# A token-major query statistic moved from ahead of the attention items into three of them

## The reference, cut to what matters

```python
q = (rms_norm(c_q, g_cq) @ w_uq).reshape(b, l, MLA_HEADS, MLA_QK)
q = rope_tail(rms_norm(q, g_q_mla), cos, sin)
...
s = jnp.einsum('bqhd,bkhd->bhqk', q_blk, k, preferred_element_type=jnp.float32) * scale
s = jnp.where(mask[None, None], s, NEG)
p = jax.nn.softmax(s, axis=-1)
return jnp.einsum('bhqk,bkhd->bqhd', p.astype(v.dtype), v)
```

## Time and profile before

| what | us |
| --- | --- |
| median of 3 runs (lowest to highest) | 1388.16 (1387.38 to 1391.67) |
| the profiled execution, device time | 1393.52 |
| its span in the profile | 1391.6 |
| PE busy | 1334.9 (96%) |
| DVE busy | 966.0 (69%) |
| ACT busy | 736.4 (53%) |
| POOL busy | 462.4 (33%) |

### The profile page before, as it was taken

How to read it: one execution, slowest core, us unless ns; L and a number is a source line. 1 busy time by engine, 2 the same in 40 slices (tenths; PEclk the granted TensorE clock), 3 DMA queues, 4 the chain that set the end, 5 groups by cost and what they waited for, 6 DMA issues and landing times.

```text
span 1391.6 us, 29208 instructions
## 1 busy us (share of the span) xinstructions
PE 1334.9 (96%) x10776; PEld 1298.5 (93%) x10776; DVE 966.0 (69%) x1446; ACT 736.4 (53%) x1224; POOL 462.4 (33%) x492
## 2 busy tenths in 40 slices
PE   5999999999999999999999999999999969999997
PEld 5787699999999999999989999999998859999996
DVE  6767567664477677555655679997578786999844
ACT  5454645444444454444545456665446844766642
POOL 3532044321111443211636324333126563333310
PEclk9998999999999999999999999999999969999998
DMA  7440045555555555555525545554554426455451
GB/s 268 150 149 32 1 152 174 186 185 184 180 181 183 180 180 183 190 187 186 195 92 183 187 175 185 183 182 169 189 202 162 137 94 223 159 191 189 143 203 53
DMA packets 34508, 230.53 MB, mean 166 GB/s; under 512 B 3838, under 2 KB 4990, under 8 KB 10662
## 3 DMA queue, kind: packets, MB, share of 16 engines
q1 hardware_dynamic: 33652, 226.47, 46.8%
q10 hardware_dynamic: 770, 2.90, 0.6%
HBM read 228.17 MB, written 1.05 MB: 165 GB/s over the span
## 4 chain that ended last, share of the span: by engine, by line
PE 77%; issue 8%; DVE 6%; ACT 4%; POOL 4%; DMA 1%; POOLq 0%; DVEq 0%; ACTq 0%; SPq 0%
PE ps L378 25%; PE ps L379 25%; PE ps L380 25%; DVE wlo L343 2%; POOL xlo L468 2%; ACT whi L338 2%; POOL ssum L474 1%; PE ps L1085 1%; DMA raw<-w 1%; DVE rstd L442 1%; DVE work L1470 1%; POOL q_mla L1857 1%; DVE work L1441 0%; PE ps L422 0%; ACT work L1752 0%
## 5 line engine op out<-in xcount | busy, mean ns | idle before, releaser
L343 DVE TENSOR_TENSOR wlo<-raw,whi 128x1024 fp32r<-128x1024 f32 (+1 forms) x448 | 546.5, 1225 | 106.2 <-ACT whi L338 105.2
L378 PE MATMUL ps<-xhi,whi 128*128 128x256 f32 (+2 forms) x2064 | 586.5, 284 | 18.5 <-DVE wlo L343 13.9
L379 PE MATMUL ps<-xlo,whi 128*128 128x256 f32 (+2 forms) x2064 | 584.6, 283 | 0.0
L380 PE MATMUL ps<-xhi,wlo 128*128 128x256 f32 (+2 forms) x2064 | 583.5, 283 | 0.0
L338 ACT ACTIVATE whi<-raw 128x1024 fp32r<-128x1024 f32 (+1 forms) x448 | 448.5, 1008 | 141.2 <-PE ps L380 136.9
L378 PEld LDWEIGHTS ps<-xhi,whi 128*128 128x128 f32 x2064 | 391.9, 190 | 23.2 <-issue 15.9
L380 PEld LDWEIGHTS ps<-xhi,wlo 128*128 128x128 f32 x2064 | 392.3, 190 | 0.0
L379 PEld LDWEIGHTS ps<-xlo,whi 128*128 128x128 f32 x2064 | 389.9, 189 | 0.3
L378 PE MATMUL ps<-hhi,whi 128*128 128x256 f32 (+1 forms) x1184 | 338.0, 285 | 7.7 <-POOL hlo L1947 7.4
L380 PE MATMUL ps<-hhi,wlo 128*128 128x256 f32 (+1 forms) x1184 | 335.7, 283 | 0.0
L379 PE MATMUL ps<-hlo,whi 128*128 128x256 f32 (+1 forms) x1184 | 335.5, 283 | 0.0
(11 more groups left out here) (262 smaller groups left out, 1314.3 us busy)
## 6 DMA issues: line engine op xcount, KB each, us to landing
raw<-w SPq DMA_DIRECT2D x184, 1024.0 KB, 4.9
raw<-w SPq DMA_DIRECT2D x40, 768.0 KB, 4.2
h<-x_fm ACTq DMA_DIRECT2D x1, 1088.0 KB, 6.4
out_fm<-h SPq DMA_DIRECT2D x8, 128.0 KB, 2.0
ws<-ws_src ACTq DMA_DIRECT2D x1, 512.0 KB, 5.0
bs<-bs_rows ACTq DMA_DIRECT2D x1, 512.0 KB, 5.8
consts<-constants ACTq DMA_DIRECT2D x1, 508.0 KB, 9.7
q_fox<-decay_rows SPq DMA_DIRECT2D x1, 340.0 KB
```

What stands on the lines that cost most here:

```text
L343: nc.vector.tensor_tensor(wlo[:, j % HLR, 0:n], raw[:, slot, col:col + n], whi[:, j % HLR, 0:n].bitcast(F32), ALU.subtract).then_inc(wlo_d ...
L378: nc.tensor.matmul(o, hi, xh, start=start, stop=False)
L379: nc.tensor.matmul(o, hi, xl, start=False, stop=False)
L380: mm = nc.tensor.matmul(o, lo, xh, start=False, stop=stop)
```

## The change

PE no longer makes the statistic ahead of the items. `q_stats(k)` makes one group, inside `turn(j)` of items 2, 3 and 4 (the third to fifth item, steps 4, 5 and 6), after the waits of `turn` and before its transposes, and writes bank 6 (columns 256 to 279) instead of bank 7. `turn(5)`, which writes bank 6 again in step 7, waits for the roots. The first `spread` waits only for the roots before (n_root 3). On ACT the two roots come in step 6, between `turned(4)` and `high`. On DVE the six scaling instructions come in step 7, behind `k_normed` and ahead of `low`. The number of products, roots and scaling instructions stays the same.

```diff
-            q_stats()
...
+                if j in (2, 3, 4):
+                    q_stats(j - 2)
+                if j == 5:
+                    pe.wait_ge(n_root, 4)
                 if kind == "d":
                     nc.tensor.transpose(ps[0:META, 6, 0:META], pr[0:META, 0:META],
...
                     if st == 0:
-                        pe.wait_ge(n_root, 4)
+                        pe.wait_ge(n_root, 3)
...
+            def query_scale():
+                c = q_scale
+                dve.wait_ge(n_root, 4)
+                nc.vector.reciprocal(q_inv[:, :, :], q_inv[:, :, :]).then_inc(c, 1)
...
                 if st < HEADS:
                     k_normed(st // 2, st % 2)
+                if st == 7:
+                    query_scale()
...
             to(p.units - 1)
-            roots(3)
...
                     turned(st - 2)
+                if st == 6:
+                    roots(3)
                 if st >= 3 and items[st - 3][0] == "h":
                     high(items[st - 3][1])
```

More of the change, by code:

```diff
@@ L872, in k_stats, with q_stats @@
                 mm.then_inc(n_ss, 1)
[L874 to L896, removed]
+            def q_stats(k):
+                if k == 0:
+                    pe.wait_ge(q_eps_step, 6)
+                m = META if k == 2 else P
+                for x in range(-1, 6):
+                    if k == 0 and x >= 0:
+                        pe.wait_ge(n_sq[3], x + 1)
+                    tile = q_eps if x < 0 else q_sq[:, x, :]
+                    if k == 2:
+                        lhs = q_sq_d[:, META * (x + 1):META * (x + 2)]
+                    else:
+                        lhs = tile[:, NQ + k * P:NQ + (k + 1) * P]
+                    if x < 0:
+                        rhs = consts[:, K_LATENT:K_LATENT + HEADS]
+                    elif Q_KIND[x] == "nope":
+                        rhs = pair_cols(Q_AT[x])
+                    else:
+                        rhs = consts[:, K_QUAD + HEADS * Q_AT[x]:K_QUAD + HEADS * (Q_AT[x] + 1)]
+                    mm = nc.tensor.matmul(ps[0:m, 6, 2 * P + k * HEADS:2 * P + (k + 1) * HEADS], lhs, rhs, start=x < 0,
+                                          stop=x == 5)
+                if k == 2:
+                    mm.then_inc(n_ss, 1)
             def turn_v(w):
@@ L1289, in _ @@
             dve.wait_ge(s("soft_set"), 3)
[L1292 to L1304, removed]
+            def query_scale():
+                c = q_scale
+                dve.wait_ge(n_root, 4)
+                nc.vector.reciprocal(q_inv[:, :, :], q_inv[:, :, :]).then_inc(c, 1)
+                dve.wait_ge(c, 1)
+                nc.vector.tensor_scalar(q_inv[:, :, :], q_inv[:, :, :], QK ** -0.5, None, ALU.mult).then_inc(c, 1)
+                dve.wait_ge(c, 2)
+                nc.vector.tensor_scalar(q_neg[:, :, :], q_inv[:, :, :], -1.0, None, ALU.mult).then_inc(c, 1)
+                nc.vector.tensor_tensor(q_diag[0:META, :], q_inv[0:META, 2, :], consts[0:META, K_DIAG:K_DIAG + HEADS],
+                                        ALU.mult).then_inc(c, 1)
+                dve.wait_ge(c, 4)
+                nc.vector.tensor_reduce(q_d[0:META, 0:1], q_diag[0:META, :], AX.X, ALU.add).then_inc(c, 1)
+                dve.wait_ge(c, 5)
+                nc.vector.tensor_scalar(q_d[0:META, 1:2], q_d[0:META, 0:1], -1.0, None, ALU.mult).then_inc(c, 1)
             def peak(j):
@@ L1514, in roots @@
                     act.wait_ge(s("soft_set"), 3)
-                    nc.scalar.activation(q_inv[:, 0:2, :], ps[:, 7, 0:2 * HEADS].rearrange("p (t h) -> p t h", t=2),
+                    nc.scalar.activation(q_inv[:, 0:2, :], ps[:, 6, 2 * P:2 * P + 2 * HEADS].rearrange("p (t h) -> p t h", t=2),
                                          ACT.Sqrt, scale=1.0 / QK, bias=par("eps3")).then_inc(s("q_root"), 1)
-                    nc.scalar.activation(q_inv[0:META, 2, :], ps[0:META, 7, 2 * HEADS:3 * HEADS], ACT.Sqrt,
+                    nc.scalar.activation(q_inv[0:META, 2, :], ps[0:META, 6, 2 * P + 2 * HEADS:2 * P + 3 * HEADS], ACT.Sqrt,
                                          scale=1.0 / QK, bias=par("eps3", rows=slice(0, META))).then_inc(n_root, 1)
```

## The result

| | kernel before | changed kernel |
| --- | --- | --- |
| median of 17 runs each (lowest to highest), us | 1389.26 (1384.97 to 1393.82) | 1390.99 (1388.74 to 1405.59) |
| ratio to before | | 1.0037 (95%: 1.0021 to 1.0053) |
| span of the profiled execution, us | 1391.6 | 1387.8 |
| attention stage in it, us | 66.22 | 69.07 |

The change makes the kernel slower by 0.37%, about 5 us, by the ratio; the plain means of the 17 runs differ by 4.1 us and the medians by 1.7. I had forecast 1.1 us, within what can't be told from no change.

What follows compares the result with a forecast made beforehand. PE, 96% busy, was taken to bound the kernel nearly everywhere. Step 7 0.45 us later, 0.35 exposed in `turn(5)` and 0.3 for the scaling made 1.1 us slower: 1389.3 us from 1388.16, range 1385.8 to 1393.8.

Steps and rivals of the forecast that it cites:

- the front of the list: Head of the items: without the statistic there, `peak(0)` comes 3.97 us earlier and step 4 on PE 3.2 us earlier.
- the groups are not hidden in steps 4 and 5: PE bounds these steps, so groups 0 and 1 add 1.61 us each, making them 5.29 and 4.87 us.
- Rival E: PE's steps 4 to 6 have hidden slack and the groups vanish in it: about 5 us faster, 1383.2; chance 6%.
- ACT and DVE: Late roots with two table loads in step 6 and scaling in step 7: 0.35 and 0.3 us exposed.
- The wait in `turn(5)`: Step 7: PE waits for the late roots behind a table load, 0.35 us exposed, bounds 0 and 1.24.
- The scaling: Step 7: six DVE instructions, about 1.1 us, delay `values` of head 4; about 0.3 us exposed, bounds 0 and 1.94.
- that of the three groups: Steps 4, 5 and 6 with the groups take 14.24 us at full clock, plus 0.95 before the clock returns.
- the clock's return near 123.0: In step 4 the clock is back at 2.4 GHz near 123.0, against 126.4 before; low until then costs 0.95 us.
- rival B: The clock falls once more among the groups for a short stretch, 1.7 us: 1391.0 us; chance 25%.
- C: The low clock holds through steps 4 and 5, 5.1 and 4.6 us more: 1394.4 to 1399.0, carried at 1395; chance 12%.
- D: The clock never falls in front of step 4, so step 3 isn't slowed: 1.1 us faster, 1387.1; chance 12%.

Runs made afterwards that it cites:

- double: The changed kernel with groups 0 and 1 made twice each, 8 columns wide: 1405.96 us, ratio 1.0139.
- fill_b: Second profile of the changed kernel plus five unread 272-column products in PE's holes of steps 1 and 2: 1395.01 us; first 1397.32 us, ratio 1.0048.
- all together: The changed kernel with groups in steps 1 to 3, groups 0 and 1 80 columns wide, sums copied out before the roots: 1385.70 us, ratio 0.9980.
- wider products: The changed kernel with each of the 21 statistic products 80 columns wide instead of 8: 1393.24 us, ratio 1.0025.

## Why the prediction was wrong

*Right: the front of the list.* `peak(0)` came at 112.33 on before's scale and step 4 at 121.26, against 112.4 and 121.1. The lead at step 4 was 124.28 - 121.26 = 3.0 us, forecast 3.2. POOL's additions did slow the small instructions of DVE beside them: the two entries of `normal` (L1336) took 0.79 and 1.03 us, and 0.22 and 0.57 in before, where they ran behind the additions.

*Right: the groups are not hidden in steps 4 and 5.* They took 1.58 us (122.59 to 124.17) and 1.63, forecast 1.61; group 2 0.44, forecast 0.40. Rival E is out.

*Right in kind: ACT and DVE.* The wait in `turn(5)` is there. The last entry of `scores(7)` began at 137.68; in step 8 the next one follows such an entry after 0.22 us, so here it could have begun at 137.90. It began at 138.52, 0.62 us exposed; I had taken 0.35. The scaling, which I had put at 0.3, held up nothing: DVE went on to `peak(8)` at once, and PE had no idle entry in steps 8 and 9. The moved roots and scaling together came out at ratio 1.0004. The drain of about 1380 ns that the Trainium skill (ScalarE: Activation LUTs, section "What ACT_TABLE_LOAD costs") has at each switch of tables is not in this trace, before or after: 138.54 + 1.28 = 139.82, and the next activation starts at 139.84. Nor is it in front of the load, where ACT worked until 138.53.

*Wrong: the clock.* The step that failed is that of the three groups: after the clock's return near 123.0 I priced steps 4, 5 and 6 at full clock, 14.24 us in all, and gave the second fall, rival B, only 25%. It came in all six profiles of the changed kernel. In the first, steps 4 to 6 took 6.68 + 6.03 + 4.12 = 16.83 us, where I had 14.24 + 0.95 = 15.19, and step 4 began 0.16 late, so that step 7 began 2.24 us after before's and not 0.45; with the 0.62 of `turn(5)` that is the growth of the stage. B priced the second fall at 1.7 us, and the comparison with the wide groups gives 1.6; B's total was +2.8. The stage grew by 2.85 us in the first profile and by 2.4 on average (68.65 over six profiles against 66.24 over two of before), and the common runs by 1.7. As evidence against B I used a stretch with PE busy for 2.23 of 3.41 us at full clock. But its products were wide, 272 and 128 columns each:

```profile
72.07 0.29 PE L379 MATMUL ps<-xlo,whi 128*128 128x272 f32 x1
...
73.46 0.66 PE L905 MATMUL ps<-consts,v_fm 128*128 128x128 f32 x4 [0.16 <-DVE k_fox L1190]
```

PE's busy time counts an 8-column product behind its weight load like any other, and the pairs of kernels with 8 and 80 columns show that columns make the difference.

*Wrong: C's size and when it comes.* I let C decide by one point, a clock still low at the start of group 0, and gave 1394 to 1399. In the runs that show it (double, fill_b) the clock was at 1.00 when group 0 began and fell in it or behind it, and then stayed low through the item work that followed. Hence up to 1408.9. In the changed kernel such runs are 6 of 33. That they are this long stretch rests on their mean clock (0.971 to 0.982, against 0.979 to 0.988 in the common ones; some 24 us more at 1.2 GHz in the mean), on the doubled variant, and on the second profile of the filler variant, not on a profile of one of them. It is likely and not shown. What decides in a given run whether the stretch is short or long was not tried.

*D and the price of the first low stretch.* I had D win by the clock staying up. The fillers, the profiles with a short first stretch and the wide products in before show that it gives little: 0, 1.0 and 1.5 us, since DVE's chain is next.

## What to carry to other kernels

Work moved into a stage where an engine has no idle entries is not hidden; in this kernel the same three groups cost nothing that could be measured in steps 1 to 3, where PE waits, and in steps 4 to 6 some 1.7 us in the common runs and 4 in the mean of all 33. Before products with few columns are placed among busy ones, ask what they do to the clock of all that follows, and try wider ones: with 128-wide weights 80 columns took the time of 8. This is to be measured in the whole program: in steps 1 and 2 it went with a gain, in steps 4 and 5 it shortened the stage and not the total. And look at the spread of many runs with their clocks: one profile had this change 3.8 us faster.

## What the runs showed of the hardware

- Fourteen fp32 instructions with 128-wide weights took 1.52 and 1.61 us from start to next start at 80 columns (111.46 to 112.98 and 114.18 to 115.79, version with all together) and 1.58 and 1.63 at 8 columns, so 72 more columns are free. With 16-wide weights they are not: 0.44 us at 8 columns, 1.07 at 80 (132.79 to 133.86, wider products).
- PE stayed at 1.2 GHz without an idle entry for 13.7 us in the doubled variant and 20.5 us in the second profile of the filler variant. Contiguous work alone does not bring the clock back at once.
- Two things brought the clock down here: 8-column products (gone with 80 columns, in the kernel before and in steps 4 and 5), and holes in PE's work at the head of the items (gone with the fillers).
- A low stretch costs by what bounds PE in it: 13.7 us cost the stage of before 1.5 to 2.1 us, in front of steps where DVE was next; in the filler variant 13.7 us more of it (20.5 against 6.8) cost 5.5 us (stage 75.0 against 69.5), where PE had no holes.
